# The gates' product of an mLSTM layer on four column groups, and its row work spread over the next product

## The chip, the cores and the metric

The kernel runs on one core of a Trainium2 chip, in one launch. The metric is the time of one execution on the device, in microseconds (us); of the kernel before there are three runs. TensorE (PE) multiplies, and loads its weights beside that (PEld); VectorE (DVE), ScalarE (ACT) and GpSimd (POOL) work on rows of 128 partitions; SyncE (SP) issues the loads of weights. Products land in PSUM, which the kernel sees as eight banks of 128 x 512 numbers in float32.

## The reference, cut to what matters

Two models follow one another on a sequence of 512 tokens with 1024 channels. The first has two attention layers and is not touched. The second has two layers of this form:

```python
proj = x @ w_in[l]
(r_q, r_k, r_v, r_g, m_qk, m_v, m_o, m_i, m_f, g_a, g_b) = jnp.split(proj, IN_OFFSETS, axis=-1)
...
qk_c = jax.nn.silu(_causal_depthwise_conv(m_qk, conv_w[l], conv_b[l])).astype(f32)
...
i_pre = m_i.astype(f32) + b_if[l, :MLSTM_HEADS].astype(f32)
f_pre = m_f.astype(f32) + b_if[l, MLSTM_HEADS:].astype(f32)
o_ml = _head_norm(_mlstm(mq, mk, mv, i_pre, f_pre), mlstm_norm_g[l]) * jax.nn.sigmoid(m_o.astype(f32))
```

m_i and m_f are the gates: four columns each, one per head, out of a projection of 1024 channels. _mlstm takes the logarithm of the sigmoid of f_pre, its running sum b over the tokens, and running maxima of i_pre - b. m_qk has 1024 columns and goes through a convolution over four tokens.

## The kernel before, in words

**Products.** A large weight comes in units of 128 x 1024 numbers, which SyncE loads into three buffers (w_raw). ScalarE rounds a unit to w_hi, VectorE subtracts and stores the rest as w_lo; activations are split the same way (h_hi, h_lo). Each product is made of three: w_hi with h_hi, w_hi with h_lo, w_lo with h_hi. gemm_fm works in panels of two tiles of 128 outputs, which fill two banks of 0 to 3 in turn; a panel of the second block's products with K = 1024 takes two units and 48 matmuls (L403). The splits run up to four units ahead.

**Order.** Each engine has a program of its own, written out in order; they meet at semaphores, here named by flow: mark(flow) counts up, after(flow) is what others wait for. The program of an engine is strictly in order. Panels.fm is the walk that ScalarE, VectorE and SyncE share: per panel it calls next_unit twice (on ScalarE a w_hi, on VectorE a w_lo), then hands out the panel's two tiles. beside and within put calls behind the first next_unit of a panel.

**The stage of the change,** once in each of the two layers of the second block: first the outputs of the retention heads (L732, banks 4 to 7, copied by ScalarE, L1087). Then the gates' product: eight float32 products of 128 channels with 36 columns each (L759), added up in bank 7; columns 0 to 3 are m_i, columns 32 to 35 are m_f, the others are zero. Then the product for m_qk, called mqk, in four panels (0 to 3). ScalarE adds the biases to the gates (row_i L1197, row_z L1198); VectorE computes row_minus (L1701); ScalarE takes Exp and Ln (L1200, L1202); VectorE does the rest of gate_rows (L1703 to L1716), which ends in row_a and row_floor. Both engines then turn to the panels: ScalarE copies the two tiles (L1208), scales them (tap 3, L1213), VectorE adds three taps for each (L1723), ScalarE applies SiLU (L1217). Behind the last mqk product TensorE transposes row_a (L767) and row_floor (L770) into bank 6, and goes on with the product mv (gemm_tm, L466), beside which the scores of the mLSTM heads run. L696 spreads a row over 128 partitions in that stage.

In the first block, the values (L560) of the even layer write two results to partitions 0 to 63 and 64 to 127 of one bank.

Of the kernel before, what the change touches and what calls it, by code (L numbers as in the profile page):

```python
# [12 lines left out]
ACT = mybir.ActivationFunctionType  # L13
AX_X = mybir.AxisListType.X

P = 128
S = 512
D = 1024
DT = D // P
# [5 lines left out]
HD = 64  # L25
DK, DV, NH2 = 128, 256, 4
# [9 lines left out]
def columns(sizes):  # L36
    at, out = 0, {}
    for name, n in sizes:
# [6 lines left out]
    [("even_norm", DT), ("odd_norm", DT), ("ffn_norm0", DT), ("ffn_norm1", DT), ("final_norm", DT), ("subln", 1)]  # L45
    + [(f"{n}{l}", c) for l in range(2) for n, c in (
        ("fconv_w", 3 * 2 * FT), ("fconv_b", 2 * FT))]
    + [("lambdas", 4 * HD)]
    + [(f"{n}{l}", c) for l in range(2) for n, c in (
        ("w_if", DT * 36), ("b_i", 1), ("b_f", 1), ("b_merge", 2 * DT), ("mconv_w", 4 * DT), ("mconv_b", DT),  # L50
        ("ret_g", DT), ("ml_g", DT), ("ln1_g", DT), ("ln1_b", DT), ("ln2_g", DT), ("ln2_b", DT))]
)

# [78 lines left out]
class Flows:  # L132
# [13 lines left out]
    def mark(self, flow, *keys, by=1):  # L146
        self.count[flow] = self.count.get(flow, 0) + by
        for key in keys:
            self.at[flow, key] = self.count[flow]
        return self.sem(flow), by  # L150

    def after(self, flow, key):
        value = self.at.get((flow, key), 0)
        assert value or not self.final, (flow, key)
        return self.sem(flow), value
# [186 lines left out]
def pe_program(e, fl, m):  # L342
    w = Once(e)
    mark, after, bank = fl.mark, fl.after, m.bank
    freed = [None] * 8
    at = {"unit": 0, "turn": 0}

    def bank_is_free(b):
        if freed[b]:
            w.wait_ge(*after(*freed[b]))  # L350
# [334 lines left out]
    for layer in range(DEPTH):  # L685
        L = str(layer)
        st = "r" + L
        ready = ("h_hi", "h_lo", st)
# [63 lines left out]
        gemm_tm("rv" + L, m.h_hi, m.h_lo, ready, lambda panel, t: ("v_act" if t % 2 else "v_dve", (L, panel, t)), begin("r"))  # L752
        finish("r")

        GB = 7
        bank_is_free(GB)
        for kt in range(DT):
            w.wait_ge(*after("x_shifted" if layer else "x_normed", (st, kt)))
            g = e.matmul(bank[GB][0:36, :], m.p("w_if" + L, kt * 36, 36), m.x[:, kt, :], start=kt == 0, stop=kt == DT - 1)  # L759
        g.then_inc(*mark("gate_rows", L))  # L760
        freed[GB] = ("row_z", L)
        gemm_fm("mqk" + L, DT, DT, m.h_hi, m.h_lo, ready, lambda f: ("mqk_copy", (L, f)))
        R = slice(0, NH2)
        w.wait_ge(*after("row_a", L))
        bank_is_free(6)
# [47 lines left out]
def act_program(e, fl, m, x_in):  # L813
    w = Once(e)
    mark, after, bank, scr, stats = fl.mark, fl.after, m.bank, m.scr, m.stats
# [17 lines left out]
    walk = Panels(next_unit)  # L833
# [338 lines left out]
    for layer in range(DEPTH):  # L1172
        L = str(layer)
        for tiles in walk.fm(DT, DT):
            for f, b in tiles:
                w.wait_ge(*after("gemm", ("tile", "qk" + L, f)))
                if f >= 2:
                    w.wait_ge(*after("cos", (L, f - 2)))
                    w.wait_ge(*after(f"halves_swapped{f % 2}", (L, f - 2)))
                e.activation(scr[f % 2][:, :], bank[b][:, :], ACT.Copy).then_inc(*mark("rope_copy", (L, f)))  # L1180
            next(shifting, None)
        for _ in shifting:
            pass
        for panel in walk.tm(iter(())):
            keep_odd(m.rv[layer], L, panel, DV)
        for h in range(NH2):
            outputs("r", h)
        w.wait_ge(*after("head_stats", ("r" + L, NH2 * TB - 1)))
        e.activation(stats[:, 32:48], stats[:, 0:32].rearrange("p (c two) -> p c two", two=2)[:, :, 1], ACT.Sqrt,
                     bias=m.eps[:, 1:2]).then_inc(*mark("head_root", "r" + L))  # L1190

        R = slice(0, NH2)
        z, _, a_row, _ = [t[layer] for t in m.row]
        bi, bf = (m.par[R, PARAMS[n + L][0]:PARAMS[n + L][0] + 1] for n in ("b_i", "b_f"))
        tmp = scr[4][R, :]
        w.wait_ge(*after("gate_rows", L))
        e.activation(a_row[R, :], bank[7][R, :], ACT.Identity, bias=bi).then_inc(*mark("row_i", L))  # L1197
        e.activation(z[R, :], bank[7][32:36, :], ACT.Identity, bias=bf).then_inc(*mark("row_z", L))  # L1198
        w.wait_ge(*after("row_minus", L))
        e.activation(tmp, tmp, ACT.Exp).then_inc(*mark("row_exp", L))  # L1200
        w.wait_ge(*after("row_exp", L))
        e.activation(tmp, tmp, ACT.Ln, bias=m.ones[R, 0:1]).then_inc(*mark("row_ln", L))  # L1202
        for tiles in walk.fm(DT, DT):
            for f, b in tiles:
                w.wait_ge(*after("gemm", ("tile", "mqk" + L, f)))
                if f >= 2:
                    w.wait_ge(*after("mqk_tap0", (L, f - 2)))
                e.activation(scr[2 + f % 2][:, :], bank[b][:, :], ACT.Copy).then_inc(*mark("mqk_copy", (L, f)))  # L1208
            for f, _ in tiles:
                w.wait_ge(*after("mqk_copy", (L, f)))  # L1210
                if f >= 2:
                    w.wait_ge(*after("mqk", (L, f - 2)))
                e.activation(scr[f % 2][:, :], scr[2 + f % 2][:, :], ACT.Identity, bias=m.p("mconv_b" + L, f),  # L1213
                             scale=m.p("mconv_w" + L, 3 * DT + f)).then_inc(*mark("mqk_tap3", (L, f)))
            for f, _ in tiles:
                w.wait_ge(*after("mqk_tap0", (L, f)))
                e.activation(m.mqk[layer][:, f, :], scr[f % 2][:, :], ACT.Silu).then_inc(*mark("mqk", (L, f)))  # L1217
        w.wait_ge(*after("a_cols", L))
        e.activation(stats[:, 80:96].rearrange("p (h t) -> p t h", h=NH2), bank[6][:, 16:32].rearrange("p (t h) -> p t h", t=TB),
                     ACT.Exp).then_inc(*mark("floor", L))  # L1220
        for panel in walk.tm(early_gates()):
            keep_odd(m.mv[layer], "m" + L, panel, DV + 1)
        for h in range(NH2):
            if h + 2 < NH2:
                gates(h + 2, 2 + h % 2)
            outputs("m", h)
        w.wait_ge(*after("m_var", L))
        e.activation(stats[:, 32:48], stats[:, 32:48], ACT.Sqrt).then_inc(*mark("head_root", "m" + L))
        gated("r", ACT.Silu)
        for panel in range(DT // 2):  # L1230
            merge_gates("r", panel)
            for _ in walk.fm(2, DT, 2 * panel):
                pass
        gated("m", ACT.Sigmoid)
        for panel in range(DT // 2):
            merge_gates("m", panel)
            for tiles in walk.fm(2, DT, 2 * panel):
                for f, _ in tiles:
                    w.wait_ge(*after("mix_sum", (L, f)))
                    e.activation(m.mix_hi[layer][:, f, :], scr[2 + f % 2][:, :], ACT.Copy).then_inc(*mark("mix_hi", (L, f)))  # L1240
        ffn(str(2 + layer), layer_norm("u" + L, "wo" + L, DT, "ln1_b" + L, True))
        shifting = layer_norm("r" + str(layer + 1), f"dn{2 + layer}", FT, "ln2_b" + L, layer < DEPTH - 1)
# [3 lines left out]
def dve_program(e, fl, m):  # L1246
    w = Once(e)
    mark, after, bank, scr, stats = fl.mark, fl.after, m.bank, m.scr, m.stats
# [437 lines left out]
    def normalise_heads(kind):  # L1686
# [3 lines left out]
        for c in range(NH2 * TB):  # L1690
# [2 lines left out]
            e.tensor_scalar(y, y, stats[:, 2 * c:2 * c + 1], stats[:, 32 + c:33 + c],  # L1693
                            ALU.subtract, ALU.mult).then_inc(*mark("headnorm", (kind + L, c)))

    def gate_rows():
        R = slice(0, NH2)
        z, lf, a_row, big_f = [t[layer][R, :] for t in m.row]
        tmp = scr[4][R, :]
        w.wait_ge(*after("row_z", L))  # L1700
        e.scalar_tensor_tensor(tmp, z, -1.0, z, ALU.mult, ALU.min).then_inc(*mark("row_minus", L))  # L1701
        w.wait_ge(*after("row_ln", L))
        e.scalar_tensor_tensor(lf, z, 0.0, tmp, ALU.min, ALU.subtract).then_inc(*mark("row_f", L))  # L1703
        w.wait_ge(*after("row_f", L))
        e.memset(z, 0.0).then_inc(*mark("row_zero", L))
        w.wait_ge(*after("row_zero", L))
        e.tensor_tensor_scan(big_f, lf, z, 0.0, ALU.add, ALU.add).then_inc(*mark("row_sum", L))
        w.wait_ge(*after("row_sum", L))
        w.wait_ge(*after("row_i", L))
        e.tensor_tensor(a_row, a_row, big_f, ALU.subtract).then_inc(*mark("row_a", L))  # L1710
        w.wait_ge(*after("row_a", L))
        e.tensor_tensor_scan(lf, a_row, a_row, 0.0, ALU.max, ALU.max).then_inc(*mark("row_scan", L))
        w.wait_ge(*after("row_scan", L))
        e.tensor_scalar(lf, lf, -1.0, None, ALU.mult).then_inc(*mark("row_max", L))
        w.wait_ge(*after("row_max", L))
        e.tensor_tensor(z, lf, big_f, ALU.subtract).then_inc(*mark("row_floor", L))  # L1716
# [96 lines left out]
    for layer in range(DEPTH):  # L1813
# [6 lines left out]
            keep_even(m.rv[layer], L, panel, DV)  # L1820
        finish("r")
        normalise_heads("r")
        gate_rows()
        for tiles in walk.fm(DT, DT):
            mqk_taps(tiles)
        w.wait_ge(*after("row_columns", L))
        e.tensor_copy(stats[:, 64:80], bank[6][:, 0:16]).then_inc(*mark("a_cols", L))
# [270 lines left out]
```

## Time and profile before

| | |
|---|---|
| median of 3 runs | 3147.22 us (3145.1 to 3147.82) |
| profiled execution | 3144.9 us |
| its span, first to last instruction | 3143.1 us |
| TensorE busy | 3094.6 us, 98% of the span |
| VectorE, ScalarE busy | 1588.9 us (51%), 1118.7 us (36%) |
| mean granted clock of TensorE | 0.996 of full speed |

A wait of TensorE for another engine is named by the line that it waited for. Busy time of TensorE is from a model of the pipeline: records of neighbouring matmuls overlap, so the distance between starts says how long one takes. A float32 product shows as two records. Lines are those of the kernel before; in the changed kernel the same statements have other numbers (L767 is L776, L770 is L779, L1208 is L1224, L1217 is L1233, L1257 is L1273, L1723 is L1742).

### The profile page before, as it was taken

The numbers are of one execution on the slowest core, as the hardware profiler recorded it, in microseconds if no ns is written. First come the engines' busy times: TensorE is split into PE (matmuls) and PEld (weight loads), VectorE is DVE, ScalarE is ACT, GpSimd is POOL, SyncE is SP. The second block draws the span as 40 slices with busy tenths as digits, with TensorE's granted clock in tenths as the row PEclk, the third lists the DMA queues.
The fourth block names the chain that finished last, engine by engine and source line by source line (L and its number), as shares of the span: only waits on it lengthen the run. The fifth ranks groups of instructions, "written<-read, shape, count | busy, mean of one in ns | idle before, by whom it ended". The sixth has DMA issues, their size and how long they took to land.

```text
span 3143.1 us, 35011 instructions
## 1 busy us (share of the span) xinstructions
PE 3094.6 (98%) x13916; PEld 2488.8 (79%) x13916; DVE 1588.9 (51%) x2353; ACT 1118.7 (36%) x1730; POOL 13.9 (0%) x24
## 2 busy tenths in 40 slices
PE   8999999999999999999999999999999999999998
PEld 7748888887688888877888888888877888888887
DVE  6575766365567652554524463334654424453324
ACT  3354443223644432334423243222334323333322
POOL 0000000000000000000000000000000000000000
PEclk9999999999999999999999999999999999999999
DMA  6302232343023223412232323333412232323321
GB/s 197 114 8 88 100 102 93 100 135 95 8 92 99 98 94 101 134 54 81 67 101 88 96 91 96 94 95 107 128 52 70 81 94 94 89 92 101 94 94 68
DMA packets 86338, 289.30 MB, mean 92 GB/s; under 512 B 11304, under 2 KB 11320, under 8 KB 85920
## 3 DMA queue, kind: packets, MB, share of 16 engines
q1 hardware_dynamic: 84016, 279.75, 28.3%
q0 software_dynamic: 1440, 6.00, 0.5%
q8 instruction: 112, 1.84, 0.2%
q10 hardware_dynamic: 720, 1.31, 0.1%
q14 instruction: 50, 0.41, 0.0%
HBM read 272.33 MB, written 2.10 MB: 87 GB/s over the span
## 4 chain that ended last, share of the span: by engine, by line
PE 94%; DVE 3%; ACT 2%; issue 1%; DMA 0%; ACTq 0%; DVEq 0%; POOLq 0%
PE banks L403 75%; PE banks L466 8%; PE banks L431 3%; PE banks L732 2%; PE banks L372 1%; PE banks L711 1%; PE banks L536 1%; PE banks L560 1%; PE banks L548 1%; PE banks L505 1%; PE banks L759 0%; PE banks L785 0%; ACT prob_e L878 0%; DVE prob_e L1401 0%; PE banks L696 0%
## 5 line engine op out<-in xcount | busy, mean ns | idle before, releaser
L1257 DVE TENSOR_TENSOR w_lo<-w_raw,w_hi 128x1024 fp32r<-128x1024 f32 (+1 forms) x512 | 612.5, 1207 | 893.7 <-ACT w_hi L825 892.4
L825 ACT ACTIVATE w_hi<-w_raw 128x1024 fp32r<-128x1024 f32 (+1 forms) x512 | 527.2, 1041 | 834.9 <-PE banks L403 751.5
L403 PE MATMUL banks<-h_hi,w_hi 128*128 128x512 f32 x2304 | 712.9, 391 | 10.2 <-DVE w_lo L1257 10.2
L403 PE MATMUL banks<-h_lo,w_hi 128*128 128x512 f32 x2304 | 710.1, 389 | 0.0
L403 PE MATMUL banks<-h_hi,w_lo 128*128 128x512 f32 x2304 | 709.9, 389 | 0.0
L403 PEld LDWEIGHTS banks<-h_hi,w_hi 128*128 128x128 f32 x2304 | 431.3, 188 | 100.1 <-issue 11.8
L403 PEld LDWEIGHTS banks<-h_lo,w_hi 128*128 128x128 f32 x2304 | 433.1, 188 | 90.2
L403 PEld LDWEIGHTS banks<-h_hi,w_lo 128*128 128x128 f32 x2304 | 432.9, 188 | 90.1
L403 PE MATMUL banks<-hid_hi,w_hi 128*128 128x512 f32 x668 | 206.5, 390 | 0.0
L403 PE MATMUL banks<-hid_lo,w_hi 128*128 128x512 f32 x668 | 205.7, 389 | 0.0
L403 PE MATMUL banks<-hid_hi,w_lo 128*128 128x512 f32 x668 | 205.6, 389 | 0.0
L403 PEld LDWEIGHTS banks<-hid_hi,w_hi 128*128 128x128 f32 x668 | 125.4, 188 | 26.8 <-issue 1.0
L403 PEld LDWEIGHTS banks<-hid_lo,w_hi 128*128 128x128 f32 x668 | 125.4, 188 | 26.1
L403 PEld LDWEIGHTS banks<-hid_hi,w_lo 128*128 128x128 f32 x668 | 125.4, 188 | 26.0
L1553 DVE SCALAR_TENSOR_TENSOR scratch<-scratch,params_sb,scratch 128x510 f32<-128x510 f32 (+1 forms) x176 | 122.3, 748 | 12.7 <-ACT scratch L983 12.7
L983 ACT ACTIVATE scratch<-scratch,params_sb 128x512 f32<-128x512 f32 x88 | 67.1, 810 | 173.0 <-DVE scratch L1566 173.0
L466 PE MATMUL banks<-w_hi,h_hi 128*128 128x512 f32 x384 | 123.7, 403 | 0.0
L466 PE MATMUL banks<-w_hi,h_lo 128*128 128x512 f32 x384 | 118.9, 391 | 0.0
L466 PE MATMUL banks<-w_lo,h_hi 128*128 128x512 f32 x384 | 118.3, 389 | 0.0
L979 ACT ACTIVATE hid_hi<-scratch 128x512 fp32r<-128x512 f32 x88 | 54.3, 633 | 166.4 <-DVE scratch L1600 106.1
L1566 DVE TENSOR_TENSOR scratch<-banks,inverse_rms 128x512 f32<-128x512 f32 x88 | 56.7, 687 | 89.5 <-PE banks L403 80.1
L466 PEld LDWEIGHTS banks<-w_hi,h_hi 128*128 128x128 f32 x384 | 70.1, 188 | 24.2 <-issue 8.9
(277 smaller groups left out, 3151.2 us busy)
## 6 DMA issues: line engine op xcount, KB each, us to landing
w_raw<-weights SPq DMA_DIRECT2D x496, 512.0 KB, 3.5
scratch<-scratch SPq DMA_DIRECT2D x128, 64.0 KB, 2.0
w_raw<-weights SPq DMA_DIRECT2D x16, 256.0 KB, 2.6
scratch<-scratch SPq DMA_DIRECT2D x32, 128.0 KB, 2.4
decay<-tables POOLq DMA_DIRECT2D x2, 1024.0 KB, 6.0
y_fm<-x_resid SPq DMA_DIRECT2D x8, 256.0 KB, 2.2
x_resid<-x_fm ACTq DMA_DIRECT2D x5, 256.0 KB, 8.2
rope<-tables POOLq DMA_DIRECT2D x2, 512.0 KB, 4.1
```

The lines of the kernel that those rows point to most:

```text
L372: mm = e.matmul(bank[b][:, :], wt[:, k, j * P:(j + 1) * P], a[:, kt + k, :], start=False, stop=kt + k == k_tiles - 1 and step == 2)
L403: mm = e.matmul(bank[b][:, :], wt[:, k, j * P:(j + 1) * P], a[:, kt, :], start=kt == 0 and step == 0, stop=kt == k_tiles - 1 and step == 2)
L431: mm = e.matmul(bank[b][:, :], weight[u % HL][:, :].rearrange("p (k c) -> p k c", k=4)[:, k, j * P:(j + 1) * P], a[:, kt, :], start=kt == ...
L466: mm = e.matmul(bank[t][:, :], a[:, kt, t * P:(t + 1) * P], wt[:, k, :], start=kt == 0 and step == 0, stop=kt == DT - 1 and step == 2)
L505: mm = e.matmul(bank[b][:, tb * P:(tb + 1) * P], every_column(m.stats[:, first + tb:first + tb + 1]), m.ident[:, :], start=tb == 0, stop=T ...
L732: o = e.matmul(bank[b][:, 0:cols], sm[:, TRI[sb] + (tb - sb) * P:TRI[sb] + (tb - sb + 1) * P], v[:, sb, h * cols:(h + 1) * cols], start=sb ...
L825: e.activation(m.w_hi[u % HL][:, 0:n], m.raw[u % RAW][:, 0:n], ACT.Copy).then_inc(*mark("w_hi", u))
L979: e.activation(m.hid_hi[int(tag)][:, f, :], scr[2 + f % 2][:, :], ACT.Copy).then_inc(*mark("hid_hi", (tag, f)))
L983: e.activation(scr[t][:, :], scr[4 + f % 2][:, :], ACT.Identity, bias=m.p("fconv_b" + tag, channels), scale=m.p("fconv_w" + tag, 2 * 2 * F ...
L1257: e.tensor_tensor(m.w_lo[u % HL][:, 0:n], m.raw[u % RAW][:, 0:n], f32(m.w_hi[u % HL][:, 0:n]), ALU.subtract).then_inc(*mark("w_lo", u))
L1553: c = e.scalar_tensor_tensor(scr[t][:, back:S], scr[u][:, 0:S - back], m.p("fconv_w" + tag, (2 - back) * 2 * FT + channels), scr[t][:, bac ...
L1566: e.tensor_tensor(scr[4 + f % 2][:, :], bank[b][:, :], m.r_bc[:, :], ALU.mult).then_inc(*mark(flow, (tag, f)))
```

## The change

The gates' weights are packed as 32 columns: 0 to 7 are the gates, the rest zero. The eight products go in turn to the four groups of 32 partitions of bank 4, two products added up in each group. ScalarE copies the bank to scratch 4, and one product with a fixed matrix "fold" of 128 x 36 adds the four groups and puts m_i to rows 0 to 3 and m_f to rows 32 to 35 of bank 5. This product stands behind the first unit of mqk. The work on the rows is taken apart: biases in panel 1 (ScalarE), row_minus in panel 2 (VectorE), Exp and Ln in panel 2 (ScalarE), the rest in panel 3 (VectorE).

```diff
@@ TensorE
-        GB = 7
-        bank_is_free(GB)
+        bank_is_free(4)
         for kt in range(DT):
+            rows = slice(kt % 4 * 32, kt % 4 * 32 + 32)
             w.wait_ge(*after("x_shifted" if layer else "x_normed", (st, kt)))
-            g = e.matmul(bank[GB][0:36, :], m.p("w_if" + L, kt * 36, 36), m.x[:, kt, :], start=kt == 0, stop=kt == DT - 1)
-        g.then_inc(*mark("gate_rows", L))
-        freed[GB] = ("row_z", L)
-        gemm_fm("mqk" + L, DT, DT, m.h_hi, m.h_lo, ready, lambda f: ("mqk_copy", (L, f)))
+            g = e.matmul(bank[4][rows, :], m.p("w_if" + L, kt * 32, 32), m.x[:, kt, :], start=kt < 4, stop=kt >= 4,
+                         skip_group_check=True)
+            if kt >= 4:
+                g.then_inc(*mark("gate_parts", (L, kt)))
+        freed[4] = ("gate_copy", L)
+
+        def fold_gate_parts():
+            w.wait_ge(*after("gate_copy", L))
+            bank_is_free(5)
+            e.matmul(bank[5][0:36, :], m.p("fold", 0, 36), m.scr[4][:, :], start=True, stop=True).then_inc(*mark("gate_rows", L))
+            freed[5] = ("row_z", L)
+
+        gemm_fm("mqk" + L, DT, DT, m.h_hi, m.h_lo, ready, lambda f: ("mqk_copy", (L, f)), beside=fold_gate_parts)
@@ ScalarE
+        w.wait_ge(*after("gate_parts", (L, DT - 1)))
+        e.activation(scr[4][:, :], bank[4][:, :], ACT.Copy).then_inc(*mark("gate_copy", L))
...
-        for tiles in walk.fm(DT, DT):
+        for tiles in walk.fm(DT, DT, within={1: gate_preactivations, 2: gate_logs}):
@@ VectorE
-        gate_rows()
-        for tiles in walk.fm(DT, DT):
+        for tiles in walk.fm(DT, DT, within={2: gate_minus, 3: gate_rows}):
             mqk_taps(tiles)
```

gate_preactivations holds the two activations with the biases, gate_logs the Exp and the Ln, gate_minus the first operation of the former gate_rows; their operations are unchanged, but for bank 5 in place of bank 7.

**TensorE, ahead of mqk, layer 0.** x_resid is the residual stream, params_sb holds the gates' weights; each row is one instruction of the program or a run of them.

```order
 L732 MATMUL banks<-rv_124,sm_ret_0_130 128x256 x2
 L732 MATMUL banks<-rv_124,sm_ret_0_130 128x256 [waits weighted]
-L759 MATMUL banks<-x_resid,params_sb 36x512 [waits out_row]
-L759 MATMUL banks<-x_resid,params_sb 36x512 x7
+L759 MATMUL banks<-x_resid,params_sb 32x512 [waits out_row]
+L759 MATMUL banks<-x_resid,params_sb 32x512 x7
 L403 MATMUL banks<-h_hi,w_hi_55 128x512 [waits w_lo,w_hi]
 L403 MATMUL banks<-h_hi,w_hi_55 128x512
```

The eight products stay where they were, with 32 columns in place of 36; the first waits for another bank's copy.

**TensorE, behind the first unit of mqk.** scratch_73 is scratch 4.

```order
 L403 MATMUL banks<-h_lo,w_hi_55 128x512 x2
 L403 MATMUL banks<-h_hi,w_lo_59 128x512 x2
+L768 MATMUL banks<-scratch_73,params_sb 36x512 [waits out_row,gate_copy]
 L403 MATMUL banks<-h_hi,w_hi_56 128x512 [waits w_lo,w_hi]
 L403 MATMUL banks<-h_hi,w_hi_56 128x512
```

The fold is new there. The transposes L767 and L770 stay right behind the last mqk product, with the same waits, as L776 and L779.

**ScalarE, panel 2 of mqk, layer 0.** w_hi rows are splits of weight units. Before:

```order
L825 ACTIVATE w_hi_58<-w_raw_53 128x1024 [waits raw_landed1]
L825 ACTIVATE w_hi_55<-w_raw_54 128x1024 [waits gemm,raw_landed2]
L1208 ACTIVATE scratch_65<-banks 128x512 [waits gemm]
L1208 ACTIVATE scratch_66<-banks 128x512
L1213 ACTIVATE scratch_63<-scratch_65,params_sb 128x512 [waits mqk,mqk_copy]
L1213 ACTIVATE scratch_64<-scratch_66,params_sb 128x512 [waits mqk,mqk_copy]
L1217 ACTIVATE mqk_134<-scratch_63 128x512 [waits mqk_tap0]
L1217 ACTIVATE mqk_134<-scratch_64 128x512 [waits mqk_tap0]
```

and changed:

```order
L834 ACTIVATE w_hi_58<-w_raw_53 128x1024 [waits raw_landed1]
L1215 ACT_TABLE_LOAD
L1215 ACTIVATE scratch_73<-scratch_73 4x512 [waits row_minus]
L1217 ACT_TABLE_LOAD
L1217 ACTIVATE scratch_73<-scratch_73,ones 4x512 [waits row_exp]
L834 ACTIVATE w_hi_55<-w_raw_54 128x1024 [waits gemm,raw_landed2]
L1224 ACTIVATE scratch_65<-banks 128x512 [waits gemm]
L1224 ACTIVATE scratch_66<-banks 128x512
L1229 ACTIVATE scratch_63<-scratch_65,params_sb 128x512 [waits mqk,mqk_copy]
L1229 ACTIVATE scratch_64<-scratch_66,params_sb 128x512 [waits mqk,mqk_copy]
L1233 ACT_TABLE_LOAD
L1233 ACTIVATE mqk_134<-scratch_63 128x512 [waits mqk_tap0]
```

The Exp and the Ln, with a table load each, stand between the two splits and thereby ahead of the panel's copies; SiLU has a table load of its own in this panel.

**VectorE, panel 3 of mqk, layer 0.** Before:

```order
L1257 TENSOR_TENSOR w_lo_60<-w_raw_52,w_hi_56 128x1024 [waits w_hi]
L1257 TENSOR_TENSOR w_lo_61<-w_raw_53,w_hi_57 128x1024 [waits w_hi]
L1723 SCALAR_TENSOR_TENSOR scratch_63<-scratch_65,params_sb,scratch_63 128x511 [waits mqk_tap3]
L1723 SCALAR_TENSOR_TENSOR scratch_64<-scratch_66,params_sb,scratch_64 128x511 [waits mqk_tap3]
L1723 SCALAR_TENSOR_TENSOR scratch_63<-scratch_65,params_sb,scratch_63 128x510 [waits mqk_tap2]
L1723 SCALAR_TENSOR_TENSOR scratch_64<-scratch_66,params_sb,scratch_64 128x510 [waits mqk_tap2]
```

and changed:

```order
L1273 TENSOR_TENSOR w_lo_60<-w_raw_52,w_hi_56 128x1024 [waits w_hi]
L1722 SCALAR_TENSOR_TENSOR row_0_146<-row_0_144,scratch_73 4x512 [waits row_ln]
L1724 MEMSET row_0_144 4x512 [waits row_f]
L1726 SCALAR_TENSOR_TENSOR row_0_150<-row_0_146,row_0_144 4x512 [waits row_zero]
L1729 TENSOR_TENSOR row_0_148<-row_0_148,row_0_150 4x512 [waits row_i,row_sum]
L1731 SCALAR_TENSOR_TENSOR row_0_146<-row_0_148 4x512 [waits row_a]
L1733 TENSOR_SCALAR row_0_146<-row_0_146 4x512 [waits row_scan]
L1735 TENSOR_TENSOR row_0_144<-row_0_146,row_0_150 4x512 [waits row_max]
L1273 TENSOR_TENSOR w_lo_61<-w_raw_53,w_hi_57 128x1024 [waits w_hi]
L1742 SCALAR_TENSOR_TENSOR scratch_63<-scratch_65,params_sb,scratch_63 128x511 [waits mqk_tap3]
L1742 SCALAR_TENSOR_TENSOR scratch_64<-scratch_66,params_sb,scratch_64 128x511 [waits mqk_tap3]
```

The seven operations of gate_rows, which stood ahead of panel 0, stand between the two splits of panel 3.

## Rows read from the trace of the kernel before

**Rows 1.** The page, part 4: shares of the chain that ended last, by engine.
```profile
PE 94%; DVE 3%; ACT 2%; issue 1%; DMA 0%; ACTq 0%; DVEq 0%; POOLq 0%
```

**Rows 2.** Waits of TensorE: engine, line, waited for; us in total, times, longest.
```profile
PE banks L759 <- ACT ret_tm L1087: 0.9, 2, 0.5
```

**Rows 3.** Timeline of TensorE, 1374 to 1485 us: start, us, engine, line, op, count, idle.
```profile
1381.33 7.06 PE L759 MATMUL banks<-x_resid,params_sb 128*36 128x512 f32 x16 [0.47 <-ACT ret_tm L1087]
1388.32 0.72 PE L403 MATMUL banks<-h_hi,w_hi 128*128 128x512 f32 x2
...
1432.08 0.40 PE L767 MATMUL banks<-ident,row 4*128 4x4 f32 x4
1432.35 0.38 PE L770 MATMUL banks<-ident,row 4*128 4x4 f32 x4
1432.66 0.73 PE L466 MATMUL banks<-w_hi,h_hi 128*128 128x512 f32 x2
...
1443.22 0.61 PE L466 MATMUL banks<-w_lo,h_hi 128*128 128x512 f32 x2
1443.77 1.12 PE L696 MATMUL banks<-row,scratch 4*128 4x512 f32 x2
1444.82 0.73 PE L466 MATMUL banks<-w_hi,h_hi 128*128 128x512 f32 x2
```

**Rows 4.** Timeline of VectorE, the work on the gates' rows, layer 0.
```profile
1393.83 0.68 DVE L1703 SCALAR_TENSOR_TENSOR row<-row,scratch 4x512 f32<-4x512 f32 x1 [3.30 <-ACT scratch L1202]
...
1396.43 0.68 DVE L1710 TENSOR_TENSOR row<-row,row 4x512 f32<-4x512 f32 x1
...
1398.84 0.68 DVE L1716 TENSOR_TENSOR row<-row,row 4x512 f32<-4x512 f32 x1
```

**Rows 5.** Timeline of ScalarE, one panel of the convolution's product and the next.
```profile
1410.42 1.09 ACT L1208 ACTIVATE scratch<-banks 128x512 f32<-128x512 f32 x2 [2.11 <-PE banks L403]
1411.39 1.52 ACT L1213 ACTIVATE scratch<-scratch,params_sb 128x512 f32<-128x512 f32 x2
1415.71 1.29 ACT L1217 ACTIVATE mqk<-scratch 128x512 f32<-128x512 f32 x2 [2.80 <-DVE scratch L1723]
1416.91 2.00 ACT L825 ACTIVATE w_hi<-w_raw 128x1024 fp32r<-128x1024 f32 x2
1421.30 1.09 ACT L1208 ACTIVATE scratch<-banks 128x512 f32<-128x512 f32 x2 [2.40 <-PE banks L403]
```

**Rows 6.** Timeline of VectorE, the same panel.
```profile
1412.25 4.10 DVE L1723 SCALAR_TENSOR_TENSOR scratch<-scratch,params_sb,scratch 128x511 f32<-128x511 f32 x6 [2.48 <-ACT scratch L1213]
1417.99 2.36 DVE L1257 TENSOR_TENSOR w_lo<-w_raw,w_hi 128x1024 fp32r<-128x1024 f32 x2 [1.65 <-ACT w_hi L825]
```

**Rows 7.** Timeline of TensorE, 165 to 175 us, two results on 64 columns each.
```profile
171.61 1.08 PE L560 MATMUL banks<-probt_e,v_e 128*64 128x512 f32 x4
172.62 1.09 PE L548 MATMUL banks<-ident,prob_e 128*128 128x128 f32 x8
```

**Rows 8.** Timeline of ScalarE, exponential and logarithm of the rows, with table loads.
```profile
1389.83 1.28 ACT L1200 ACT_TABLE_LOAD   x1
1391.12 0.63 ACT L1200 ACTIVATE scratch<-scratch 4x512 f32<-4x512 f32 x1
1391.77 1.28 ACT L1202 ACT_TABLE_LOAD   x1
1393.07 0.73 ACT L1202 ACTIVATE scratch<-scratch,ones 4x512 f32<-4x512 f32 x1
```

**Rows 9.** Windows: from:to, length, busy us of each engine, PEclk, DMA share, GB/s.
```profile
152.00:157.80 5.80, 2.87 (x16) 0.93 (x12) 5.73 (x27) 3.24 (x12) 0.00 (x0) 0.99 0.14 57
157.80:164.60 6.80, 6.04 (x26) 4.11 (x26) 4.69 (x20) 4.83 (x18) 0.00 (x0) 0.50 0.00 0
...
823.80:826.70 2.90, 0.45 (x5) 0.41 (x5) 0.42 (x1) 2.89 (x9) 0.00 (x0) 1.00 0.00 0
826.70:830.10 3.40, 3.40 (x17) 2.73 (x16) 2.24 (x5) 1.16 (x4) 0.00 (x0) 0.50 0.00 0
```

More of the change, by code:

```diff
@@ L47 @@
         ("fconv_w", 3 * 2 * FT), ("fconv_b", 2 * FT))]
-    + [("lambdas", 4 * HD)]
+    + [("lambdas", 4 * HD), ("fold", 36)]
     + [(f"{n}{l}", c) for l in range(2) for n, c in (
-        ("w_if", DT * 36), ("b_i", 1), ("b_f", 1), ("b_merge", 2 * DT), ("mconv_w", 4 * DT), ("mconv_b", DT),
+        ("w_if", DT * 32), ("b_i", 1), ("b_f", 1), ("b_merge", 2 * DT), ("mconv_w", 4 * DT), ("mconv_b", DT),
         ("ret_g", DT), ("ml_g", DT), ("ln1_g", DT), ("ln1_b", DT), ("ln2_g", DT), ("ln2_b", DT))]
@@ L1195, in act_program, with gate_preactivations, gate_logs @@
         tmp = scr[4][R, :]
[L1196 to L1202, printed above, removed]
-        for tiles in walk.fm(DT, DT):
+        def gate_preactivations():
+            w.wait_ge(*after("gate_rows", L))
+            e.activation(a_row[R, :], bank[5][R, :], ACT.Identity, bias=bi).then_inc(*mark("row_i", L))
+            e.activation(z[R, :], bank[5][32:36, :], ACT.Identity, bias=bf).then_inc(*mark("row_z", L))
+        def gate_logs():
+            w.wait_ge(*after("row_minus", L))
+            e.activation(tmp, tmp, ACT.Exp).then_inc(*mark("row_exp", L))
+            w.wait_ge(*after("row_exp", L))
+            e.activation(tmp, tmp, ACT.Ln, bias=m.ones[R, 0:1]).then_inc(*mark("row_ln", L))
+        for tiles in walk.fm(DT, DT, within={1: gate_preactivations, 2: gate_logs}):
             for f, b in tiles:
@@ L1694, in normalise_heads, with gate_minus @@
                             ALU.subtract, ALU.mult).then_inc(*mark("headnorm", (kind + L, c)))
+    def gate_minus():
+        z, tmp = m.row[0][layer][0:NH2, :], scr[4][0:NH2, :]
+        w.wait_ge(*after("row_z", L))
+        e.scalar_tensor_tensor(tmp, z, -1.0, z, ALU.mult, ALU.min).then_inc(*mark("row_minus", L))
     def gate_rows():
@@ L1699, in gate_rows @@
         tmp = scr[4][R, :]
-        w.wait_ge(*after("row_z", L))
-        e.scalar_tensor_tensor(tmp, z, -1.0, z, ALU.mult, ALU.min).then_inc(*mark("row_minus", L))
         w.wait_ge(*after("row_ln", L))
@@ L2068 @@
     put("subln", tiles(a["odd_subln"][0]))
+    fold = np.zeros((P, 36))
+    for group in range(4):
+        fold[group * 32 + np.arange(8), [0, 1, 2, 3, 32, 33, 34, 35]] = 1
+    put("fold", fold)
     put("lambdas", np.concatenate([a["odd_lambda_" + n][0] for n in ("q1", "k1", "q2", "k2")])[None, :])
@@ L2074 @@
         put("fconv_b" + L, tiles(a["ffn_conv_b"][l]))
-        w_if = np.zeros((D, 36), np.float32)
-        w_if[:, 0:4] = a["w_in_2"][l][:, 6144:6148]
-        w_if[:, 32:36] = a["w_in_2"][l][:, 6148:6152]
-        put("w_if" + L, w_if.reshape(DT, P, 36).transpose(1, 0, 2).reshape(P, -1))
+        w_if = np.zeros((D, 32), np.float32)
+        w_if[:, 0:8] = a["w_in_2"][l][:, 6144:6152]
+        put("w_if" + L, w_if.reshape(DT, P, 32).transpose(1, 0, 2).reshape(P, -1))
         params[0:4, PARAMS["b_i" + L][0]] = a["b_if_2"][l][0:4]
```

## The prediction

> **What bounds the kernel now.** I read four views. The chain that ended last comes first: TensorE holds 94% of it [rows 1]. An instruction moves the end only if it takes TensorE time in this chain, or makes TensorE wait. Then the waits of TensorE: the gates' product waited twice, 0.9 us in all, for a copy out of its bank [rows 2]. Next the timeline of TensorE in layer 0 of the second block. The gates' product starts at 1381.33 and the convolution's product (mqk) at 1388.32; the latter runs to 1432.08 without a hole. There the transposes of the gates' rows follow (L767, L770), and at 1432.66 the next product, mv [rows 3]. So TensorE pays 6.99 us for eight narrow products, and nothing for the row work: VectorE has row_floor ready at 1398.84 + 0.68 = 1399.5 [rows 4], 32 us before L770 asks for it. Last, ScalarE and VectorE inside one panel of mqk, because that is where the row work goes [rows 5, 6].
>
> **Removed: the wait and the serial product.** The first gate product now goes to bank 4, which is emptied three copies earlier than bank 7, so the 0.47 us ahead of it go [rows 3]. With the 6.99 us that is 7.46 us per layer.
>
> **Added: eight products on four column groups.** No row shows four groups. The nearest is L560: its two results go to two groups of 64 columns, with different data streaming. Four records with 512 elements start at 171.61 and the next line starts at 172.62 [rows 7]. That is 1.01 us for two products, where products of this length one behind the other take 0.87 each (6.99 / 8). So two groups run side by side, for 0.15 us more than one product. Four groups in two rounds make 2 x 0.86 + 0.15 = 1.87 us. The lower bound is 1.72; the upper one is 6.99, nothing side by side; side by side in pairs only gives 3.6. I take 1.87, since L560 loses so little.
>
> The Trainium skill (TensorE: Matmul & The Clock Gate, "Measured speedup vs the span model") gives 3.07x for four row tiles and 2.38x for three column tiles. By the first of them the eight products would take an estimated 2.3 us and the sum below would be 0.4 us higher per layer; it has no figure for four column tiles.
>
> **Added: the fold.** One product (L768) between two units of mqk. The nearest is L696, also one f32 product of 512 elements between full-size ones: from the pair at 1443.22 (0.45 long by its neighbours, 10.88 us for 24 of them) to the pair at 1444.82 it adds 1.15 us [rows 3]. I take 1.15, with bounds 0.86 and 1.4. Its operand, the copy of the partial sums, is not late: the parts end near 1382.7, a 128x512 copy takes 0.55 [rows 5], and the fold comes a unit later, 5.47 us (43.76 / 8 by rows 3). About 4.8 us of cover remain.
>
> Up to here: -7.46 + 1.87 + 1.15 = -4.44 us per layer.
>
> **Moved: the row work, and the wait that it makes.** L776 (before L767) still needs row_a, and L779 (before L770) row_floor, at the same place, right behind the last mqk product. But VectorE now starts gate_rows inside panel 3. I count from C, the start of a panel's first copy (L1208): C1 = 1410.42, C2 = 1421.30, so panels are 10.88 apart, C3 = 1432.18, and TensorE reaches the transposes at C3 - 0.10 [rows 3, 5]. In a panel of before, SiLU runs from C + 5.29 to C + 6.58, the two w_hi splits from C + 6.49 to C + 8.49 (the first ends near C + 7.5), and VectorE's w_lo starts at C + 7.57, 1.18 each [rows 5, 6].
> - Panel 2 begins with gate_logs. ScalarE: first w_hi to C1 + 7.5, table load 1.28 to 8.8. The Exp waits for row_minus, which VectorE does behind its w_lo (7.57 to 8.8, then 0.7: 9.5). Exp 0.63, table load 1.28, Ln 0.73 [rows 8], second w_hi 1.0: C1 + 13.1. So the copies of panel 2 start 2.2 us late (10.88 was due). ScalarE's slack in a panel was 10.88 - 8.49 = 2.4 us and the logs take 4.6.
> - Panel 3: VectorE's gate_rows stands behind a w_lo, whose w_hi stands behind panel 2's SiLU. The w_lo ends 7.57 + 1.2 = 8.8 after panel 2's copies start, 2.2 late: C2 + 11.0 = C3 + 0.1. From there row_a takes 3.28 us (1393.83 to 1396.43 + 0.68) and row_floor 5.69 [rows 4].
> - TensorE stands from C3 - 0.10 to C3 + 3.5 for row_a, does L776, and gets row_floor at C3 + 5.9. Before, L770 began at C3 + 0.17 [rows 3]. That is 5.7 us of stall per layer. Queued behind it is the whole mv product.
>
> Bounds of the stall: 3.5 if the logs delay nothing; 7 if row operations run 20% longer beside other traffic. Behind it on VectorE are a w_lo (its unit is needed two mv units later, some 11 us) and panel 3's taps; both shift with mv, so I add nothing for them. The fourth table load and the copy of the parts lie on ScalarE in time already counted, or idle.
>
> **The clock.** A stall of this length may cost twice. Three stretches of this trace have TensorE at half clock (1.2 instead of 2.4 GHz), each behind a thin one: after 5.8 us with 2.87 busy it stood at 0.50 for 6.8 us; after 2.9 us with 0.45 busy, for 3.4 us; in each TensorE was busy [rows 9] (the third, at 779, repeats the first). Half clock on a dense product costs half of the stretch: 1.7 or 3.4 us. Here 6 us pass with some 0.5 us busy, then mv follows at full density. Bounds 0 (the slow stretch falls into the stall) and 3.4; I take 2.5, between the two.
>
> The Trainium skill (TensorE: Matmul & The Clock Gate, "Why this matters for your kernels") asks for no idle gap over about 3 us between bursts of matmuls, and so speaks against this change; the trace agrees, with a drop after a gap even shorter.
>
> **Sum.** -4.44 + 5.7 + 2.5 = +3.76 us per layer; layer 1 has the same order, so +7.5 for two. The profiled execution took 3144.9 us (span 3143.1, 1.8 around it), which gives 3152.4. The median of the runs is 2.3 higher, at 3147.22: **3154.7 us**.
>
> **Rivals.**
> - No clock loss: the slow stretch lies in the stall, or doesn't come. Then +2.5 in all: 3149.7. For it: this stall is twice as long as the gap ahead of the 3.4 us stretch, so the slow time may begin inside it. Against: in all three stretches TensorE was busy in nearly all of the slow time [rows 9].
> - The logs delay nothing, stall 3.5: -0.9 per layer, plus a short clock loss of 1.7 or none: 3145.4 to 3148.8. It needs ScalarE to have 2.2 us more slack than rows 5 show.
> - The groups don't run side by side, so the change doesn't do what it says: in pairs +1.7 per layer, 3158; serial +5.1, 3165. For it: nothing here shows 32 columns or four streams. Against: L560.
> - The other side, faster: the row work stays hidden and TensorE gets the whole -4.44 twice: 3138.3. It decides at one point: gate_rows must start by C3 - 5.8, which is C2 + 5.1. The w_hi that it stands behind can't start before C2 + 6.49, even without a delay by the logs. Only a VectorE that took the rows ahead of its w_lo could do it, and its order doesn't.
>
> **How the numbers follow.** The forecast's case 0.58, with its own range 3151 to 3159 (clock 0.7 to 3.4 per layer, eight products 1.87 to 2.3); no clock loss 0.17; short stall 0.07; groups in pairs or serial 0.12; faster 0.06. A measurement tells 0.2%, 6.3 us, from no change: 3140.9 to 3153.5 is the same. About a fifth of the forecast's case lies below 3153.5, so same = 0.12 + 0.17 + 0.07 = 0.36; slower = 0.46 + 0.12 = 0.58; faster 0.06. The range: 3148 to 3160 leaves out faster, the best of the short stalls, and serial groups.
>
> **What would show it.** In the changed profile: L759's eight products in about 1.9 us instead of 6.99; L768 with no wait, about 1.15 us; copies of panel 2 (L1224) about 2.2 us later against their matmuls than those of panel 1; L776 waiting near 3.5 us and L779 near 2 us for VectorE rows, in both layers; a stretch at half clock around or behind them. I am wrong if TensorE goes into mv with no hole, if the hole is there with the clock at full, or if L759 still takes over 3 us.

## The result and the profile after

| | before | after |
|---|---|---|
| median, 20 runs each | 3145.15 us (3142.62 to 3148.70) | 3151.78 us (3150.46 to 3154.16) |
| ratio of the runs | | 1.0020, 95% interval 1.0015 to 1.0026 |
| profiled execution, its span | 3144.9, 3143.1 us | 3151.61, 3149.8 us |
| mean granted clock | 0.996 | 0.994 |

The change costs 6.6 us by the medians, 6.7 by the spans. First the waits of TensorE in the changed kernel (line, waited for: us in total, times, longest):

```profile
PE banks L776 <- DVE row L1729: 6.4, 2, 3.2
...
PE banks L779 <- DVE row L1735: 4.0, 2, 2.0
```

The wait of [rows 2] is gone from this list, and two new ones stand in it, once per layer each. Now the timeline of TensorE, layer 0, for [rows 3]:

```profile
1375.77 4.70 PE L732 MATMUL banks<-rv,sm_ret 128*128 128x256 f32 x21
1380.40 1.92 PE L759 MATMUL banks<-x_resid,params_sb 128*32 128x512 f32 x16
1382.25 0.73 PE L403 MATMUL banks<-h_hi,w_hi 128*128 128x512 f32 x2
...
1387.37 0.61 PE L403 MATMUL banks<-h_hi,w_lo 128*128 128x512 f32 x2
1387.92 1.05 PE L768 MATMUL banks<-scratch,params_sb 128*36 128x512 f32 x2
1388.90 0.72 PE L403 MATMUL banks<-h_hi,w_hi 128*128 128x512 f32 x2
...
1430.50 0.41 PE L776 MATMUL banks<-ident,row 4*128 4x4 f32 x4 [3.21 <-DVE row L1729]
1432.90 0.58 PE L779 MATMUL banks<-ident,row 4*128 4x4 f32 x4 [2.00 <-DVE row L1735]
1433.42 1.22 PE L466 MATMUL banks<-w_hi,h_hi 128*128 128x512 f32 x2
1434.44 1.05 PE L466 MATMUL banks<-w_hi,h_lo 128*128 128x512 f32 x2
...
1446.49 1.12 PE L696 MATMUL banks<-row,scratch 4*128 4x512 f32 x2
```

The eight products take 1.85 us from L759 to mqk, and the fold stands without a wait. Then two holes, and mv's first pairs of records follow each other after 1.02 and 0.85 us. Before, the same pairs, from the one at 1432.66 in [rows 3] on, took 0.57 and 0.46:

```profile
1433.23 0.63 PE L466 MATMUL banks<-w_hi,h_lo 128*128 128x512 f32 x2
1433.69 0.62 PE L466 MATMUL banks<-w_lo,h_hi 128*128 128x512 f32 x2
```

So mv starts at half clock. The windows (from:to, length, busy us of PE, PEld, DVE, ACT, POOL; then PEclk, DMA share, GB/s), to be read against [rows 9]:

```profile
1427.20:1430.80 3.60, 0.39 (x5) 0.31 (x4) 3.33 (x6) 2.48 (x4) 0.00 (x0) 1.00 0.43 146
1430.80:1437.60 6.80, 4.80 (x16) 3.82 (x16) 6.73 (x10) 0.28 (x1) 0.00 (x0) 0.50 0.27 80
1437.60:1444.00 6.40, 6.40 (x30) 5.27 (x29) 2.92 (x5) 4.46 (x6) 0.00 (x0) 1.00 0.08 11
```

The clock fell inside the stall, 3.5 us after its start, and came back 4.2 us after mv had begun. In layer 1 it fell 5.0 us after the stall's start and came back 5.7 us after mv had begun. What TensorE waited for stands on ScalarE and VectorE; ScalarE first, panels 1 to 3, for [rows 5, 8]:

```profile
1405.57 1.09 ACT L1224 ACTIVATE scratch<-banks 128x512 f32<-128x512 f32 x2 [1.13 <-PE banks L403]
...
1412.05 1.04 ACT L834 ACTIVATE w_hi<-w_raw 128x1024 fp32r<-128x1024 f32 x1
1413.11 1.28 ACT L1215 ACT_TABLE_LOAD   x1
1414.97 0.63 ACT L1215 ACTIVATE scratch<-scratch 4x512 f32<-4x512 f32 x1 [0.58 <-DVE scratch L1715]
1415.62 1.28 ACT L1217 ACT_TABLE_LOAD   x1
1416.91 0.72 ACT L1217 ACTIVATE scratch<-scratch,ones 4x512 f32<-4x512 f32 x1
1417.54 1.04 ACT L834 ACTIVATE w_hi<-w_raw 128x1024 fp32r<-128x1024 f32 x1
1418.49 1.04 ACT L1224 ACTIVATE scratch<-banks 128x512 f32<-128x512 f32 x2
...
1423.75 1.29 ACT L1233 ACTIVATE mqk<-scratch 128x512 f32<-128x512 f32 x2 [1.50 <-DVE scratch L1742]
1424.94 1.99 ACT L834 ACTIVATE w_hi<-w_raw 128x1024 fp32r<-128x1024 f32 x2
1427.32 1.09 ACT L1224 ACTIVATE scratch<-banks 128x512 f32<-128x512 f32 x2 [0.39 <-PE banks L403]
```

Panel 2's copies start 12.92 us after panel 1's where 10.88 was due: 2.04 late. And VectorE in panel 3, for [rows 4, 6]:

```profile
1426.02 1.23 DVE L1273 TENSOR_TENSOR w_lo<-w_raw,w_hi 128x1024 fp32r<-128x1024 f32 x1 [1.65 <-ACT w_hi L834]
1427.16 0.67 DVE L1722 SCALAR_TENSOR_TENSOR row<-row,scratch 4x512 f32<-4x512 f32 x1
...
1429.76 0.68 DVE L1729 TENSOR_TENSOR row<-row,row 4x512 f32<-4x512 f32 x1
...
1432.17 0.68 DVE L1735 TENSOR_TENSOR row<-row,row 4x512 f32<-4x512 f32 x1
```

gate_rows starts (L1722, 1427.16) when TensorE has just finished mqk, behind a split that waited for ScalarE's. row_a ends at 1430.44, and L776 starts 0.06 later.

**A measure for the experiments.** Executions of one kernel differ by 3 us and more, also for reasons outside of this stage (one is seen below, in e3). So I also take the length of the stage from each trace: from the end of L732 (its start and its length in its row) to the start of the first L696, both layers added. Before: 62.91 + 62.96 = 125.87. After: 66.02 (1446.49 - 1380.47) + 66.72 = 132.74, which is 6.87 more, and the spans differ by 6.7. All that the change costs lies in this stage.

### The profile page after: what moved, and what is told of

It reads as the page before. It is cut to its first block, busy times and chain, and to the rows that moved or that the text cites. A ratio compares the mean times of both kernels' runs of the same rounds, so it can differ in the third digit from the quotient of the medians.

```text
span 3149.8 us, 35027 instructions
## 1 busy us (share of the span) xinstructions
PE 3091.8 (98%) x13920; PEld 2489.8 (79%) x13920; DVE 1588.4 (50%) x2353; ACT 1121.6 (36%) x1734; POOL 13.8 (0%) x24
## 4 chain that ended last, share of the span: by engine, by line
PE 93%; DVE 4%; ACT 2%; issue 1%; DMA 0%; ACTq 0%; DVEq 0%; POOLq 0%
PE banks L403 74%; PE banks L466 9%; PE banks L431 3%; PE banks L732 2%; PE banks L372 1%; PE banks L711 1%; PE banks L536 1%; PE banks L560 1%; PE banks L548 1%; DVE scratch L1742 1%; PE banks L505 1%; PE banks L794 0%; ACT prob_e L887 0%; DVE prob_e L1417 0%; PE banks L696 0%
```

## The experiments

Theory A: the product gives what was forecast, and the late rows take more than that, by a stall and by the clock. Rival B: the column groups or the fold cost something themselves. Rival C: the row work makes TensorE wait wherever it stands.

**e1: the row work early, the product as changed.** Against the changed kernel:

```diff
-        for tiles in walk.fm(DT, DT, within={1: gate_preactivations, 2: gate_logs}):
+        for tiles in walk.fm(DT, DT, within={0: lambda: (gate_preactivations(), gate_logs())}):
...
-        for tiles in walk.fm(DT, DT, within={2: gate_minus, 3: gate_rows}):
+        for tiles in walk.fm(DT, DT, within={0: gate_minus, 1: gate_rows}):
```

> The changed kernel with the row work placed earlier: biases, row_minus, Exp and Ln in panel 0 of mqk, gate_rows in panel 1 of VectorE; the product on four groups and the fold as they are. Theory A (the product gives about 4.5 us per layer, and all that was lost is the late rows: stall 5.4 and half clock 2): no wait of TensorE at L776 or L779, clock at full, 2 x -4.5 = -9 us against the kernel before, about 3136 on a chip where before takes 3145. Rival B (the four-group product or the fold costs something elsewhere, and the stall only shows it): at most 3 us faster than before. Rival C (the row work makes TensorE wait wherever in mqk it stands, by late copies out of the banks): a new wait at the first mv products for copies, -9 plus some 3 us.

Measured: 3136.01 us against 3145.03 of before, ratio 0.9971 (0.9961 to 0.9981). Stage: 116.97, -8.90. TensorE at the end of mqk, in e1:

```profile
1427.53 0.41 PE L776 MATMUL banks<-ident,row 4*128 4x4 f32 x4
1427.81 0.38 PE L779 MATMUL banks<-ident,row 4*128 4x4 f32 x4
1428.12 0.73 PE L466 MATMUL banks<-w_hi,h_hi 128*128 128x512 f32 x2
```

No hole. And VectorE's last row operation in e1:

```profile
1409.37 0.68 DVE L1735 TENSOR_TENSOR row<-row,row 4x512 f32<-4x512 f32 x1
```

row_floor is ready 17.8 us before L779 starts. The product is worth the whole -4.45 us per layer, so rival B falls, and rival C does for this placement. This kernel is faster than the one before and than the changed one.

**e2: only the late row work, on the product of before.** Its edit is the two within tables of the change and gate_minus taken out of gate_rows, in the kernel before.

> The kernel before (eight products of 36 columns in bank 7, no fold) with only the row work moved, as late as in the changed kernel. Theory A: the same stall of 5.4 us and half clock of about 2 us per layer with nothing to pay for it, +15 us against before, about 3160. Rival B (the stall is a matter of the new product): no more than +3 us.

Measured: 3161.22 us, ratio 1.0052 (1.0039 to 1.0065). Stage: 140.36, +14.49. Its waits are those of the changed kernel:

```profile
PE banks L767 <- DVE row L1717: 6.4, 2, 3.2
...
PE banks L770 <- DVE row L1723: 3.7, 2, 1.9
```

The stall and the half clock need nothing of the new product. The two parts add up: -8.90 by e1 and +14.49 by e2 make +5.6, measured are +6.87. The 1.3 between them is mostly the clock: from the first mv product to L696, e2 takes 12.54 and 13.00 us and the changed kernel 13.07 and 13.76, where before took 11.1.

**e3: the clock kept up through the stall.** keep_clock(n) issues n matmuls on constant operands into bank 7; nobody uses their result.

```diff
+        keep_clock(14)
         w.wait_ge(*after("row_a", L))
...
+        keep_clock(8)
         w.wait_ge(*after("row_floor", L))
```

> The changed kernel with dummy matmuls of TensorE (128x512, bfloat16, into bank 7) in the two waits: 14 ahead of L776, 8 ahead of L779; nobody uses their result. Theory A: the stall stays (L776 and L779 start where they did), the clock stays at full, and the 2 us per layer of half clock are gone: -4 us against the changed kernel, about +2.5 against before. If the half clock cost nothing, the time is that of the changed kernel, +6.6. If the dummies last longer than the waits, up to +1 us.

Measured: 3148.99 us, ratio 1.0010 (1.0001 to 1.0018). Stage: 127.79, +1.92 against before and -4.95 against the changed kernel. The timeline of e3:

```profile
1430.05 2.97 PE L482 MATMUL banks<-masks_bf 128*128 128x512 bf16 x13
1433.20 0.40 PE L777 MATMUL banks<-ident,row 4*128 4x4 f32 x4 [0.18 <-DVE row L1731]
1433.54 1.90 PE L482 MATMUL banks<-masks_bf 128*128 128x512 bf16 x8
1435.61 0.41 PE L781 MATMUL banks<-ident,row 4*128 4x4 f32 x4 [0.17 <-DVE row L1737]
1435.95 0.73 PE L466 MATMUL banks<-w_hi,h_hi 128*128 128x512 f32 x2
1436.52 0.62 PE L466 MATMUL banks<-w_hi,h_lo 128*128 128x512 f32 x2
```

The stall is as long as it was, the clock stays at 1.00, and 2.5 us per layer come back. That is the clock's share, measured apart from the stall's. By the medians only 2.8 us come back; in e3 the profiled execution has another stretch at half clock of 3.4 us, in the first block, which the profiles before and after have not (a window of e3, PEclk 0.50):

```profile
849.00:852.40 3.40, 3.40 (x13) 2.37 (x12) 1.22 (x2) 0.84 (x2) 0.00 (x0) 0.50 0.00 0
```

It costs an estimated 1.7 us (half of 3.4) of the 2.1 between the two readings, if the other executions of e3 have it too, which isn't known. The profiled executions of e4, e6 and e7 have such a stretch of 3.4 us too, from 848 or 849 on; those of e1, e2, e5 and e8 have none. The spans of the four that have it are 1.7 to 2.5 us longer than the span before plus the change of their stage; the others are from 1.0 us shorter to 0.2 longer. So the stage, and not the median, is the measure for differences of 2 us. What decides whether an execution has this stretch is open.

**e4: the logs a panel earlier, gate_rows where the change has it.** Edit: {0: gate_preactivations, 1: gate_logs} and {1: gate_minus, 3: gate_rows}.

> The changed kernel with biases in panel 0, row_minus, Exp and Ln in panel 1, so that they delay panel 1's copies and not panel 2's; gate_rows stays in panel 3. Theory A (gate_rows is late by its place behind SiLU and the split, and 2.0 us more by the logs): stall 5.4 - 2.0 = 3.4 us per layer, half clock 1 to 3 us: -2 to -4 us for both layers against the changed kernel or, with half clock as before, about 3148. Rival (the place alone decides): stall 5.4 as in the changed kernel.

Measured: 3149.03 us, ratio 1.0010 (1.0001 to 1.0019). Stage: 129.05, -3.69 against the changed kernel. Its waits:

```profile
PE banks L779 <- DVE row L1735: 4.0, 2, 2.0
...
PE banks L776 <- DVE row L1729: 2.4, 2, 1.2
```

The wait for row_a is 2.0 us per layer shorter, as much as the logs' delay. Of the stall of 5.4 us, 2.0 come from the logs, and 3.4 from gate_rows' place behind SiLU and the split: in e8, which differs from e4 only in gate_rows a panel earlier, the stall is gone.

**e5, e6, e7: the column groups alone, on e1.** One line differs:

```diff
-            rows = slice(kt % 4 * 32, kt % 4 * 32 + 32)
+            rows = slice(0, 32)                              # e5
+            rows = slice(kt % 2 * 32, kt % 2 * 32 + 32)      # e6
+            rows = slice(kt // 2 * 32, kt // 2 * 32 + 32)    # e7
```

(the start and stop flags follow, and in e5 and e6 the unused rows of fold are zero).

> Run e1 with all eight gate products on the first group of 32 columns (the copy and the fold stay, the fold's other rows are zero). Theory A (what the groups save is only that four products stream at once): L759 takes 6.9 us instead of 1.85, +5.0 us per layer, +10 against e1, about 3146. Rival (the narrower weights or the other bank save the time, not the groups): L759 below 4 us, time within 3 us of e1.

> Run e1 with the gate products in turn on two groups of 32 columns. Theory A: four rounds of 0.86 and 0.15, L759 takes 3.6 us, +1.75 per layer, +3.5 against e1, about 3139.5. If products of 32 columns overlap less than those of 64 did: up to 5 us.

> Run e1 with the same four groups in another order: products 0 and 1 on group 0, 2 and 3 on group 1, and so on, so that neighbours in the program share a group. Theory A (products start in program order, and one that finds its group busy holds up those behind it): each second product waits for its neighbour, so about five products' time, 4.3 us in place of 1.85, +2.5 per layer, +5 against e1. Rival (the engine takes a later product for a free group out of turn): 1.85 us and no difference.

TensorE in e5, then e6, then e7, the eight products and the first of mqk:

```profile
1380.51 7.05 PE L759 MATMUL banks<-x_resid,params_sb 128*32 128x512 f32 x16
1387.49 0.74 PE L403 MATMUL banks<-h_hi,w_hi 128*128 128x512 f32 x2
```

```profile
1382.85 3.63 PE L759 MATMUL banks<-x_resid,params_sb 128*32 128x512 f32 x16
1386.41 0.73 PE L403 MATMUL banks<-h_hi,w_hi 128*128 128x512 f32 x2
```

```profile
1382.40 1.94 PE L759 MATMUL banks<-x_resid,params_sb 128*32 128x512 f32 x16
1384.27 0.73 PE L403 MATMUL banks<-h_hi,w_hi 128*128 128x512 f32 x2
```

6.98, 3.56 and 1.87 us. Medians 3148.35, 3141.61 and 3138.55, ratios 1.0006 (0.9997 to 1.0015), 0.9985 (0.9976 to 0.9995), 0.9976 (0.9967 to 0.9985); stages +1.39, -5.54, -8.91. The stages of e5 and e6 came as Theory A had them: the time goes with the number of groups. The medians of all three are some 2 us over what was expected and over their stages; e7's stage equals that of e1, so those 2 us lie elsewhere in the kernel. The profiled executions of e6 and e7 have the extra slow stretch of e3; that of e5 has none, and it took 3146.23 us, 2.1 below e5's median. Theory A was wrong for e7: neighbours on the same group cost nothing, so the rival holds. The section on the kernel before calls the program of an engine strictly in order; for TensorE's products on different column groups that isn't so, since in strict order the eight of e7 need five rounds of 0.86 us. Their 16 records start four at a time, 0.43 to 0.45 us apart, as in the changed kernel.

**e8: the change's own spread, one panel earlier.** Edit: {0: gate_preactivations, 1: gate_logs} and {1: gate_minus, 2: gate_rows}.

> The changed kernel with its spread kept, each piece one panel earlier: biases in panel 0, row_minus, Exp and Ln in panel 1, gate_rows in panel 2. Theory A says no wait at L776 or L779 and full clock. By the panels' rows gate_rows then pushes panel 2's taps and SiLU late, and with them the copies of panel 3 out of banks 2 and 3, by some 2.2 us; mv needs bank 2 about 1.8 us after its start, so it waits some 1.5 us per layer: -9 + 3 = -6 against before, about 3139, 3 us behind e1. If the copies are in time: as e1, 3136.

Measured: 3140.54 us, ratio 0.9983 (0.9974 to 0.9992). Stage: 119.45, -6.42. ScalarE and TensorE in e8:

```profile
1426.94 1.99 ACT L834 ACTIVATE w_hi<-w_raw 128x1024 fp32r<-128x1024 f32 x2
...
1428.84 1.06 ACT L1224 ACTIVATE scratch<-banks 128x512 f32<-128x512 f32 x2
1429.46 0.98 PE L466 MATMUL banks<-w_hi,h_hi 128*128 128x512 f32 x2 [0.70 <-ACT scratch L1224]
```

The rows are in time (L776 at 1426.51 without a wait), but their 5.7 us on VectorE push ScalarE's copies of panel 3 back, to 2.3 us after the end of mqk, and mv waits for their bank. From mv to L696 it takes 12.39 us in place of 11.12: 1.27 us per layer, where 1.5 was expected. This is rival C for this placement. The clock stays at full.

## Why the prediction was right

The forecast added 7.5 us to the profiled execution and came to 3154.7; the change cost 6.6 us and the median is 3151.78. Of the 2.9 us between the two, 2.1 come from the median of before, which the prediction took from three runs (3147.22) and which is 3145.15 over twenty, and 0.9 from the change itself. By the prediction's own bound (slower from 3153.5 on) the time lies in what it called the same, to which it gave 0.36 against 0.58 for slower; the 6.6 us that were measured, 0.21%, are just over the 0.2% that it took as the least to be told from no change. The upper end of the forecast's own range, 3159, doesn't follow from the two spans given with it: 2 x (0.9 + 0.43) above 3154.7 is 3157.4. The mechanism came term by term.

Per layer, in us; "measured" is from the traces of before and after, the clock from its own records in both layers:

| term | predicted | measured |
|---|---|---|
| wait and eight products | -7.46 + 1.87 = -5.59 | -5.68 |
| fold | +1.15 | +1.22 |
| stall at L776 and L779 | +5.7 | +5.44 |
| half clock | +2.5 | +2.14 and +2.82 |
| sum | +3.76 | +3.11 and +3.76 (the stages) |

- **The product.** Wait and products took 0.47 + 6.99 of TensorE before and take 1.85 less 0.07 of overlap after. What two groups of 64 columns did [rows 7], four of 32 do. But the 0.15 us of that term isn't a price of running side by side: on one group (e5) eight products also take 6.98, which is 0.12 more than 16 records at the 0.429 us from one start to the next. The Trainium skill (TensorE: Matmul & The Clock Gate, "Measured speedup vs the span model") has 3.07x for four row tiles, another way to divide the array; these four column groups give 6.98 / 1.85 = 3.8x, over eight products. For this case the measurement decides.
- **The fold.** From the first mqk product to the transposes e1 takes 44.98 us, and before took 43.76 [rows 3]: 1.22, near the 1.15 of L696.
- **The stall.** Without the clock, from e3: L777 stands 3.27 us later behind its mqk than in e1 (48.25 against 44.98 from the first mqk product), and mv starts 2.75 us after it in place of 0.58; 3.27 + 2.17 = 5.44. The forecast had the logs' delay at 2.2 and it was 2.04; both waits came where it had put them. Its own terms (row_floor ready 5.69 us after C3 + 0.1) give 5.6 rather than 5.7. Its upper bound let row operations run 20% longer, which no run shows: gate_rows took 5.69 us before and in the changed kernel.
- **The clock.** The changed kernel loses 0.17 in L779 (2.92 against 2.75 of e3) and 1.97 and 2.65 from mv to L696 (13.07 and 13.76 against 11.10). With the 0.17 that is about half of the slow time that mv saw, 4.2 and 5.7 us. The prediction gave no clock loss 0.17 and its reason was half true: the slow time did begin inside the stall. But it lasted for 6.8 us, as behind the first thin stretch of [rows 9], and not for 3.4. The forecast's 2.5 was not worked out but put between its bounds of 0 and 3.4. That a loss came and why was right; that the mean of the two layers is 2.48 is luck. The prediction also held against this rival that TensorE was busy in all three slow stretches of before. The trace has a fourth, which [rows 9] don't show: at the end of the program, where TensorE has nothing left to do from 3133.1 on, the clock fell at 3137.6. So a fall inside an idle time could be seen beforehand.
- **The rivals.** Groups in pairs or serial: no, by L759 itself. Short stall: no; e4 is that kernel, its stage +3.2 against before, where the rival had at most +1.6, since e4's clock fell all the same, for 6.8 us in each layer. Faster: not in this order, since the w_lo ahead of gate_rows began at 1426.02, 9.6 us after the time at which panel 2's copies were due (1405.57 + 10.88).

## What to carry to other kernels

A step with two operands on four rows of 512 elements takes VectorE as long as one on 128 rows (0.68 us, as each of the six taps of [rows 6]); when a chain of such steps (here 9.7 us over two engines, from the first table load of [rows 8] to the end of [rows 4]) is moved, count from the consumer backwards, with all that stands ahead of each piece in its engine's order. The gain of a shorter product and the loss of a later operand are separate and add up; the same product with its rows two panels earlier turns +6.6 us into -9.0. A stall of TensorE is to be priced with the slow clock behind it, here 2.5 us on top of 5.4, which dummy matmuls in the hole give back.

## What the runs showed of the hardware

- Neighbours in program order on one column group cost nothing (e7: 1.87 us for eight products; in the order of the change 1.85). That products for free groups are taken while an earlier one waits for its group is read from this time, since the records don't name the group; in strict order it would have been 4.3 us.
- Float32 products of 32 columns in four groups stream four different operands at once, each at the rate that one product alone has (two rounds of 0.86 in 1.85 us).
- In a hole of 5.6 us with 0.4 us busy the clock went to 1.2 GHz 3.5 us (layer 0) and 5.0 us (layer 1) after the hole's start. In e2's hole, about as long, it was 2.3 and 3.4 us, and in e4's hole of 3.6 us 2.8 and 2.4 us. It stayed there for 6.8 us in both layers of all three kernels. e8's wait of 0.7 us in mv did not bring it down.
